# Eight of twelve blocks of a modulation vector: their products with the weights' rows made on VectorE, TensorE adding over the partitions alone

## What is computed

```python
mod_l = jnp.split((jax.nn.silu(c) @ w_ada[i] + b_ada[i])[:, None, :], 6, axis=-1)
mod_c = jnp.split((jax.nn.silu(c_ctx) @ w_ada[i] + b_ada[i])[None, None, :], 6, axis=-1)
...
hc = modulate(xc, mod_c[0], mod_c[1])        # of mod_c only these two are used: there is one layer
hl = modulate(xl, mod_l[0], mod_l[1])
```

## Time and profile before

| | |
|---|---|
| median of 3 runs | 1613.26 us (1612.24 to 1613.64) |
| the profiled execution's own time | 1614.68 us, of which the profile's span is 1612.8 us |
| busy, share of the span | PE 97%, DVE 49%, ACT 38%, POOL 30% |
| granted TensorE clock, mean | 0.995 |
| feed-forward steps, layer 0 and 1 | end at 281.9 us and at 621.9 us of the span |
| loads of `w_ada` | issued from 147.2 to 602.0 us |

### The profile page before, as it was taken

One profiled execution on the slowest core, in us unless ns is written; L12 is line 12 of the kernel. 1 busy time (PEld: TensorE's weight loads), 2 busy tenths in 40 slices (PEclk: granted clock), 3 DMA queues, 4 the chain that ended last, 5 costly groups with the idle time before them and its releaser, 6 DMA issues.

```text
span 1612.8 us, 24052 instructions
## 1 busy us (share of the span) xinstructions
PE 1566.7 (97%) x9726; PEld 1182.5 (73%) x9726; DVE 783.9 (49%) x1291; ACT 612.4 (38%) x1110; POOL 480.6 (30%) x318
## 2 busy tenths in 40 slices
PE   7999999999999999999999999999999999999987
PEld 6889899868889998888787888998644444444442
DVE  5654434246564332479767776446433333233223
ACT  4653444345553443455446665332211111111110
POOL 4432655434334544300126665353300000000000
PEclk9999999999999999999999999999999999999999
DMA  8644996537439986443427666957899999999994
GB/s 284 213 157 131 256 268 223 180 96 271 143 87 304 263 261 222 141 105 105 130 53 221 198 192 204 301 141 293 353 405 425 420 422 424 422 422 424 421 422 179
DMA packets 249972, 410.50 MB, mean 255 GB/s; under 512 B 7685, under 2 KB 196689, under 8 KB 228480
## 3 DMA queue, kind: packets, MB, share of 16 engines
q1 hardware_dynamic: 242864, 379.09, 67.7%
q10 hardware_dynamic: 3584, 19.86, 3.1%
q0 software_dynamic: 3408, 9.95, 1.7%
HBM read 407.72 MB, written 1.15 MB: 254 GB/s over the span
## 4 chain that ended last, share of the span: by engine, by line
PE 86%; DMA 6%; DVE 3%; issue 1%; POOL 1%; ACT 1%; SPq 0%; ACTq 0%; DVEq 0%; POOLq 0%
PE ps L144 84%; DMA arena<-in_w_expert_gate 2%; DMA arena<-in_w_expert_up 2%; PE ps L146 2%; DVE arena L154 1%; DVE arena L150 1%; DMA ring<-in_w_out 1%; POOL split_r L150 1%; DMA ring<-in_w_gate_up 1%; ACT split_r L148 1%; DVE split_r L150 1%; DMA rows<-in_b_s 0%; POOL arena_r L150 0%; ACT arena L148 0%; DVE arena_r L150 0%
## 5 line engine op out<-in xcount | busy, mean ns | idle before, releaser
L144 PE MATMUL ps<-arena_r,split_r 128*128 128x256 f32 (+1 forms) x2984 | 460.1, 288 | 2.6 <-POOL split_r L150 2.6
L150 POOL TENSOR_TENSOR split_r<-ring,split_r 128x1024 fp32r<-128x1024 f32 (+1 forms) x142 | 328.8, 2317 | 276.0 <-ACT split_r L148 247.0
L144 PEld LDWEIGHTS ps<-arena_r,split_r 128*128 128x128 f32 x2984 | 393.4, 188 | 23.2 <-issue 17.1
L148 ACT ACTIVATE split_r<-ring 128x1024 fp32r<-128x1024 f32 (+1 forms) x293 | 295.9, 1020 | 253.0 <-PE ps L144 183.6
L150 DVE TENSOR_TENSOR split_r<-ring,split_r 128x1024 fp32r<-128x1024 f32 (+1 forms) x151 | 225.8, 1497 | 290.6 <-ACT split_r L148 290.4
L144 PE MATMUL ps<-split_r,arena_r 128*128 128x512 f32 (+1 forms) x1520 | 340.8, 378 | 7.6 <-issue 3.1
L144 PEld LDWEIGHTS ps<-split_r,arena_r 128*128 128x128 f32 x1520 | 276.0, 189 | 54.4 <-issue 12.1
L144 PE MATMUL ps<-arena 128*64 128x512 f32 (+8 forms) x1232 | 303.3, 471 | 4.6 <-DVE arena L160 3.7
L144 PE MATMUL ps<-ring,arena 128*64 128x512 f32 (+2 forms) x688 | 226.1, 575 | 2.6 <-DMA rows<-in_w_expert_gate 0.9
L144 PE MATMUL ps<-hhh_r,split_r 128*128 128x256 f32 (+1 forms) x976 | 228.5, 322 | 0.0
L144 PEld LDWEIGHTS ps<-arena 128*64 128x64 f32 (+2 forms) x1232 | 120.9, 150 | 114.2 <-issue 101.2
(11 more groups left out here) (160 smaller groups left out, 1299.2 us busy)
## 6 DMA issues: line engine op xcount, KB each, us to landing
ring<-in_w_gate_up SPq DMA_DIRECT2D x88, 512.0 KB, 7.4
ring<-in_w_in SPq DMA_DIRECT2D x57, 512.0 KB, 5.4
arena<-in_w_ada SPq DMA_DIRECT2D x24, 1024.0 KB, 7.4
arena<-in_w_expert_gate SPq DMA_DIRECT2D x12, 2048.0 KB, 26.1
ring<-in_w_down SPq DMA_DIRECT2D x22, 1024.0 KB, 4.8
ring<-in_w_expert_up SPq DMA_DIRECT2D x11, 2048.0 KB, 25.1
ring<-in_w_expert_down SPq DMA_DIRECT2D x11, 2048.0 KB, 26.9
ring<-in_w_in SPq DMA_DIRECT2D x28, 768.0 KB, 5.9
```

Source lines behind the costliest of these rows:

```text
L144: made = e.matmul(*a, **k)
L148: made = e.activation(*a, **k)
L150: made = e.tensor_tensor(*a, **k)
```

## The change

Units 4 to 11 (eight of twelve) no longer have `ada_products` on PE and `products_kept` on DVE. DVE makes them: eight instructions of 128x512, one for each chunk of 128 rows: the first multiplies with the column `cs[:, k, 0:1]`, the other seven multiply and add to `AD` (`scalar_tensor_tensor`). They go in three parts (3, 3 and 2 instructions) behind `gated` in the steps a, a+1 and a+2, each waiting for the one before. PE adds over the partitions at the end of step a+3, with a matrix of ones in place of the selecting one; both columns then hold `c`'s sum. Units 0 to 3 stay as they are. `ADA_AT` puts six units into each layer (before: five and seven): in layer 0 the four of PE two steps apart, then two of DVE three apart; in layer 1 six of DVE three apart, steps 3 to 20. SP loads weights up to unit m+6 for DVE's units and still waits for `("am", u)`, which now comes with the eighth instruction. POOL's wait in layer 1 is for unit 5 instead of 4.

```diff
-        ADA_AT = ({4: 0, 8: 1, 12: 2, 16: 3, 20: 4}, {3: 5, 6: 6, 9: 7, 12: 8, 15: 9, 18: 10, 20: 11})
+        ADA_AT = ({4: 0, 6: 1, 8: 2, 10: 3, 12: 4, 15: 5}, {3: 6, 6: 7, 9: 8, 12: 9, 15: 10, 18: 11})
+        ADA_BY_DVE = 4
+        ada_begun = lambda l, m: [u for a, u in ADA_AT[l].items() if u < ADA_BY_DVE and a == m]
+        ada_step = lambda l, m: [(u, m - a) for a, u in ADA_AT[l].items() if u >= ADA_BY_DVE and a <= m < a + 3]
+        ada_ended = lambda l, m: [u for a, u in ADA_AT[l].items() if m == a + (1 if u < ADA_BY_DVE else 3)]
...
-                        t.matmul(bk, C("selbc"), AD[u % 2], True, True).then_inc(*sig(s_mm, ("ada", u)))
+                        t.matmul(bk, ones, AD[u % 2], True, True).then_inc(*sig(s_mm, ("ada", u)))
...
-                        made = t.matmul(bk[:, 2 * c:2 * c + 2], AD[u % 2][:, tok(c)], C("selc"), True, True)
+                        made = t.matmul(bk[:, 2 * c:2 * c + 2], AD[u % 2][:, tok(c)], C("selc") if u < ADA_BY_DVE else ones[:, 0:2], True, True)
...
-                    if m - 1 in ADA_AT[l]:
-                        ada_sums(ADA_AT[l][m - 1])
-                    if m in ADA_AT[l]:
-                        ada_products(ADA_AT[l][m])
+                    for u in ada_ended(l, m):
+                        ada_sums(u)
+                    for u in ada_begun(l, m):
+                        ada_products(u)
...
+            def modulation(u, part):
+                o = AD[u % 2]
+                row = lambda k: AW[:, k // 4, k % 4, :]
                 if u // 2 in (3, 4):
-                    then(v.copy(in_fours(AD[u % 2]), by_four(B("am", u))), ("am", u, "kept"))
-                else:
-                    then(v.copy(AD[u % 2], B("am", u)), ("am", u, "kept"))
+                    o, row = in_fours(o), lambda k: by_four(AW[:, k // 4, k % 4, :])
+                if part == 0:
+                    v.wait_ge(*at("cs"))
+                    v.wait_ge(*at("ada", u - 2))
+                for k in range(*((0, 3), (3, 6), (6, 8))[part]):
+                    if k % 4 == 0:
+                        v.wait_ge(*at("ada_in", u, k // 4))
+                    if k == 0:
+                        then(v.tensor_scalar(o, row(k), cs[:, k, 0:1], None, ALU.mult))
+                    else:
+                        v.wait_ge(*v.latest)
+                        then(v.stt(o, row(k), cs[:, k, 0:1], o, ALU.mult, ALU.add), *([("am", u), ("am", u, "kept")] if k == 7 else []))
...
-                    if m - 1 in ADA_AT[l]:
-                        modulated_by(ADA_AT[l][m - 1])
-                    if m in ADA_AT[l]:
-                        products_kept(ADA_AT[l][m])
+                    for u in ada_ended(l, m):
+                        modulated_by(u)
+                    for u in ada_begun(l, m):
+                        products_kept(u)
+                    for u, part in ada_step(l, m):
+                        modulation(u, part)
...
-                    g.wait_ge(*at("am", 4))
+                    g.wait_ge(*at("am", 5))
...
-                    load_to(up[m + 5])
+                    load_to(up[m + (5 if u < ADA_BY_DVE else 7)])
                     y.wait_ge(*at("am", u))
```

More of the change, by code:

```diff
@@ L2011, in products_kept @@
                     v.wait_ge(*at("ada", u - 2))
+                then(v.copy(AD[u % 2], B("am", u)), ("am", u, "kept"))
+            def modulation(u, part):
+                o = AD[u % 2]
+                row = lambda k: AW[:, k // 4, k % 4, :]
                 if u // 2 in (3, 4):
-                    then(v.copy(in_fours(AD[u % 2]), by_four(B("am", u))), ("am", u, "kept"))
-                else:
-                    then(v.copy(AD[u % 2], B("am", u)), ("am", u, "kept"))
+                    o, row = in_fours(o), lambda k: by_four(AW[:, k // 4, k % 4, :])
[10 more added lines that the diff above has]
+                        then(v.stt(o, row(k), cs[:, k, 0:1], o, ALU.mult, ALU.add), *([("am", u), ("am", u, "kept")] if k == 7 else []))
             def modulated_by(u):
```

## The result

The changed kernel takes 1616.79 us (median of 8 runs, 1614.39 to 1619.77) against 1613.01 (8 runs of the kernel before, 1609.84 to 1616.83): 3.8 us more, a ratio of 1.0025 with a 95% interval of 1.0014 to 1.0036. The forecast was 4.9 us more. The execution that was profiled (1614.39) is the fastest of the eight.

A forecast was written before the change was run, and what follows sets the result against it. PE was taken to bound the kernel, with DVE's and POOL's serial chain already as long as its step; +5.4 in layer 1, -1.15 and +0.6 in layer 0 gave +4.9 us, predicted 1618.5, range 1606 to 1630.

The forecast's parts named there:

- The step: Feed-forward steps with DVE's multiply-adds: 7.5 or 6.4 us in units 6 to 9 (strided write), plain 6.5 or 5.7.
- the wait for the load: First step of a DVE unit: DVE waits for `w_ada`, making the step 8.5 us instead of 7.5, plain 7.3.
- the turns between DVE and POOL: Feed-forward steps: DVE and POOL instructions that read and write SBUF alone exclude each other, whole instructions long; a waiting one goes next.
- One sign: Layer 1, steps 3 to 20: silus at the steps' ends some 7 us apart, not 5.76.
- Layer 1: Layer 1's steps from PE's step end at 499.8: 127.5 us against 122.1 before, a loss of 5.4 us.
- Layer 0: Layer 0's loop: 1.15 us gained, 0.6 charged for sums of unit 5 that come late.
- the lead of split quarters: Layer 0: quarters split over a step ahead cover the 3.1 us by which two plain units exceed PE's need.
- the rival of a dear read: Units 6 to 9: the strided read costs too, 28 multiply-adds at 0.4 more, +11 us, 1629; chance 0.13.
- The rival's floor of 116.0 us: Layer 1: if DVE's work is hidden, DMA queues, 0.95 busy over 122.1 us, limit the loop to 116.0, -6.1 us.
- cover after all: Rival: DVE's instructions fit into gaps or strided ones take 0.9 us or less; time 1606; chance 0.17.
- The late weights: Rival: SP stands behind the mark for three steps, 2 us a unit more in layer 1, 1628; chance 0.07.
- the expected 16.3 us: PE's work removed: eight times 2.04 us of products, seven in layer 1 and one in layer 0.

The follow-up runs named there:

- the sum in PSUM: Changed kernel with the running sum of units 4 to 11 held in a PSUM bank, only the eighth instruction writing AD in SBUF: 1600.34 us, 0.9915.
- all `lo` by DVE: Changed kernel with DVE making the `lo` of all quarters in steps 2 to 21 of both layers, POOL none: 1603.9 us, 0.9953.
- the plain write: Changed kernel with units 6 to 9 written to AD in plain order, PE reading AD with a stride of four elements: 1603.84 us, 0.9952.
- the fast kernels: Changed kernel without six of eight products in units 4 to 11, 1599.82 us; and with sum in PSUM, first half ahead, all `lo` by DVE, 1595.11 us.
- the last experiment: Changed kernel with the running sum in PSUM, the next unit's first half loaded ahead and all `lo` by DVE: 1595.11 us, 0.9897.
- the first half ahead: Changed kernel with the next unit's first half of `w_ada` loaded as soon as the fourth of eight instructions is done: 1608.6 us, 0.9982.

## Why the prediction was right

**The step.** Forecast from rows: 7.5 us with three strided instructions, 6.4 with two, 8.5 with the wait for the load, and plain 6.5, 5.7 and 7.3. Measured from end to end of `gated` in the changed kernel: 7.3 to 7.5, 6.3, 8.4 to 8.8, and plain 6.2, 5.6 and 7.2. The sum from `gated(3)` to `gated(21)` was 127.6 us; it is 629.87 - 503.56 = 126.3. The steps' lengths are shown in the trace; that the turns between DVE and POOL make them is shown by the sum in PSUM, all `lo` by DVE and the plain write, which all shorten the turns in different ways, and of which the second lengthens DVE's work. One sign held only in part: the silus are some 7 us apart up to step 16, but 5.8 to 6.6 in the last five steps. There the chain is PE's again:

```profile
588.30 38.67 PE ps L144 x299
```

PE, set back by its waits, works without a pause from 588.30 on and comes to the last sums at 626.27, just as DVE's last multiply-add ends (626.22). So the count of DVE's and POOL's work gives the right length for the end of the loop too, though in these steps PE doesn't wait for it.

**Layer 1.** Forecast a loss of 5.4 us. PE began the last sums at 626.27, which is 126.3 after step 3's end; 122.1 before: 4.2 lost. The mechanism was right and the term 1.2 too large, as each plain step was taken 0.1 to 0.3 too long.

**Layer 0.** Forecast 1.15 gained and 0.6 given back, so 0.55 gained; nothing was. The loop takes 131.9 us both times. What PE saves behind the loop doesn't reach layer 1, which begins 336.2 and 336.3 us after layer 0's first silu. Between them, near 361 us, the granted clock fell to half (1.2 GHz) for 3.4 us in this execution and not in that of before, which makes the last half microsecond unreadable. That the lead of split quarters hides two plain units there was right: PE's steps are 5.76 (6.6 with sums) but for one of 5.92. That the total came out near the forecast owes something to luck: layer 1 lost 1.2 us less than forecast and layer 0 gained 0.55 less, and the two partly cancel.

**Prices.** The strided multiply-add was taken as 1.1 us with nothing for the strided read. Alone it takes 1.18 (pairs of 2.36 to 2.37), and 1.17 to 1.19 where the sum is read from PSUM; so the rival of a dear read, which took 1.5, is refuted. The plain tensor_scalar was put at 0.5 from rows of 64 and 128 elements and is 0.48; the strided one is 0.81, not 1.1 (561.28 in the kernel with all `lo` by DVE). The estimate from the Trainium skill's cycle rule ("VectorE: DVE Perf Modes", section "The TRN2 errata"), 0.33 us, lies below the measured 0.48; at one element a cycle the same rule gives an estimated 0.59, so the measured time lies between the two. With its output in PSUM the instruction takes 0.75.

**What was wrong.** The rival's floor of 116.0 us for the DMA queues: loops of 110.7 and 106.6 us refute it. The step that failed is "the same bytes must move". The change takes one unit of `w_ada` out of layer 1, so the bytes of these steps are 2.1 MB fewer; at the rate of before, 291 GB/s, the floor comes to an estimated 108.8 us. The windows of the fast kernels moved 31.0 and 30.6 MB (not all of the difference is `w_ada`, since the loads of the following weights also fall on either side of a window's edge), and the queues had a share of 0.95 and 1.00. The product of share and time was sound; it has to be taken with the bytes of the changed kernel. The rival itself, cover after all, didn't come true in the change; its time of 1606 only set the lower end of the range. The late weights were no cost in the change (0.7 us of ACT's waiting in layer 1); with the sum in PSUM ACT waited 4.9 us for them, in a kernel that was faster all the same.

**Where the expected 16.3 us went.** PE's work did fall; in layer 1 PE then waited 13.2 us, 5.5 for POOL's `lo` and 7.7 with its sums for DVE's last multiply-add, since a loop that was PE's became that of DVE and POOL together. And PE was busy for 113.3 us there, where the same matmuls take 106.6 at full clock in the last experiment: the mean granted clock of 0.96 accounts for some 5 us of that (0.04 x 126.5), told below.

## What to carry to other kernels

Before work is moved to VectorE, add its SBUF-only instructions to GpSimd's in the same stretch, each at full length, as if they were on one engine, and set that sum against the step; busy shares of 41% and 53% hid a chain that was already as long as TensorE's step. A running sum kept in PSUM takes VectorE's multiply-adds out of that count at hardly any cost in their own time (0.756 us against 0.750; only the unit's first instruction pays, 0.75 against 0.48). A floor by DMA has to be worked out with the bytes that the changed kernel moves in the stage, not with those of the kernel before. A load into a single buffer should be asked for by halves, as soon as each half is free, above all where an idle moment lets another engine take the turn.

## What the runs showed of the hardware that was not expected

The granted TensorE clock, full in layer 1's loop before, fell to half for 3.4 us three times in the changed kernel's (mean 0.96 in the window above), after stretches in which PE had waited between matmuls. There DVE and POOL set the pace and hid most of it: the step in which DVE stood for `w_ada` took 8.83 us from `gated` to `gated` twice with the fall and 8.35 once without. With the first half ahead it came twice, the second time for some 7 us, in a step of 10.48 us (two stretches of 4 us in that step, PE busy throughout):

```profile
564.00:568.00 4.00, 4.00 (x21) 4.00 (x22) 3.97 (x5) 0.42 (x2) 2.13 (x1) 0.56 0.69 228
568.00:572.00 4.00, 4.00 (x23) 4.00 (x23) 3.93 (x3) 2.00 (x2) 3.86 (x2) 0.58 1.17 310
```

A wait that an engine seems to bear can thus cost it again afterwards. In the kernels whose PE never waited there, the clock stayed full. But not every wait was followed by a fall: in the changed kernel PE was busy for 2.10 of the 4 us before 544 and for 2.11 of the 4 us before 568, and the clock fell only behind the first; with all `lo` by DVE PE waited 6.7 us in the loop without a fall, with the plain write 1.9 us with one. So no rule for it comes out of these runs. And a 128x128 float32 operand that PE loads with a stride of four elements makes eight small matmuls take 1.91 us, instead of 0.95 to 1.05.
